# Moving a load, a normalization and two DMA groups within the queues of a 3-block transformer kernel

## Chip, cores and metric

The kernel runs on one core of a Trainium2 chip. The metric is the device time of one execution in microseconds (us), lower is better; three executions of a kernel are compared by their median. All matmuls run on TensorE (PE), elementwise work on VectorE (DVE), ScalarE (ACT) and GpSimd (POOL), and DMAs are issued from the queues of SyncE (SP), ScalarE and GpSimd.

## What is computed

One sequence of 512 tokens, width 1024, goes through two mixers (a gated delta rule, then a short convolution) and a third block: compressed, selected and windowed attention with a pooling and a gating branch, cross attention to a memory of 256 rows, and a gated feed-forward net. Everything is float32. Two places matter here:

```
# gated delta rule, chunks of 64 tokens, per head
a_mat = tril(kb k^T * decay, -1);  u, w = solve(I + a_mat, vb), solve(I + a_mat, kb * exp(g))
for each chunk: v_new = u - w S; o = q S + (qk) v_new; S = S * decay + k^T v_new
o = rms_norm(o, norm_w) * silu(z);  y = o @ w_out

# third block
x = x + rms_norm(concat(attention, pool, gate) @ w_out_2)
m = rms_norm(mem_2)            # 256 rows of 1024
x = x + rms_norm(cross_attention(rms_norm(x) @ w_mq, m @ w_mk, m @ w_mv) @ w_mo)
```

## The kernel before

Activations lie transposed in SBUF (8 tiles of 128 channels by 512 tokens). Each weight matrix is cut into slabs of 256 columns (128 partitions by 2048 floats, 1 MB). SP loads the slabs in a fixed order into a ring of two slots. For most of them the float32 product is made of three products of rounded parts: ACT writes the high part `w_hi` of a slab (`split_hi`, L1516), DVE or POOL writes the low part `w_lo = ring - w_hi` (`split_lo`, L2114 and L2847), and PE multiplies hi by hi, hi by lo and lo by hi (L740 to L742). `w_hi` and `w_lo` have two places each, so the high part of slab n+2 can only be written when PE has used up slab n.

Every engine runs its own instructions in the order in which the program issues them. Semaphores tie the engines together; a wait in a queue, the SP queue too, holds up all that stands behind it.

**The delta rule** works on 4 groups of 4 heads (g = 0 to 3). In each group ACT writes the decay factors (L1746), DVE multiplies them into `A_T` (L2408, counted by `a_ready`) and `QK_T` (L2410). The diagonal blocks of 16 by 16 of A are then inverted by DVE in another layout: four DMAs from SP (L556) and four from ACT (L1752) write the blocks to `blocks_d` in DRAM, SP reads them back (L558), DVE inverts them (`invert_blocks`, L2373 and L2376), SP writes `inverses_d` (L564), and four DMAs each from SP (L569) and ACT (L1766) bring the inverses back. PE waits for those and goes on with transposes (L1063). From g = 1 on, the RMS norm of the outputs of the group before is worked in between: ACT sums squares of its last chunk (`out_squares`, L1699), DVE makes means of them (`out_means`, L2340 and L2345), ACT takes the roots (`out_roots`, L1709 and L1711), and DVE scales the outputs (`scaled_outs`, L2354), before it starts `invert_blocks(g)`. PE turns the scaled outputs (L987) once DVE has also read its banks (`vb_ready`, L2418).

**The attention's output projection** has 4 slabs, called XOUT to XOUT+3. Its 8 output tiles (`mix_proj(c)`, c = 0 to 7) use one slab for two tiles. The first 4 tiles are accumulated at L1367 to L1369, from `mix_start` on, while the attention still runs; the last 4 are at L740 to L742. After tiles 3 to 6 PE transposes two tiles each of the memory rows (L1403); the first of these waits for `mem_scaled`. The memory's norm consists of the load `mem_rows` (L666), two squares with row sums, a Ln and an Exp on ACT (L1995 to L1999, ends with `mem_rstd`), and two scalings on DVE (L2757, L2758, end with `mem_scaled`). The load writes into a part of SBUF that the attention uses, so it waits for `attT_out`, the end of the attention. `post_norm` squares and copies the eight output tiles as PE finishes them (ACT L1534 and L1548, DVE L2150 and L2153); at even tiles it first runs `ahead`, the split of slab XOUT+2 or XOUT+3, and after each tile `beside(k)`.

Of the kernel before, what the change touches and what calls it, by code (L numbers as in the profile page):

```python
# [8 lines left out]
D = 1024  # L9
P = 128  # L10
KD = D // P
NT = S // P
# [79 lines left out]
def build(nc, x, pre_norm_w, post_norm_w, gdn_w_in, gdn_conv_w, gdn_A_log, gdn_dt_bias, gdn_norm_w, gdn_w_out,  # L92
# [5 lines left out]
    ALU, ACT, AX = mybir.AluOpType, mybir.ActivationFunctionType, mybir.AxisListType  # L98
    ds = bass.ds
    ctx = ExitStack()  # L100
    with ctx:
# [24 lines left out]
        small = sb("small", P, 64)  # L126
        inv_count = sb("inv_count", P, 32)[:, :]
        eps = small[:, 0:1]
# [83 lines left out]
        v_of = [xT[:, 4:8, :], gate_out[:, 12:16, :]]  # L212
# [100 lines left out]
        XOUT = len(plan)  # L313
# [141 lines left out]
        MT, HD = MEM // P, D // MH  # L455
# [4 lines left out]
        mem_rows, at = cut(at, MT, D)  # L460
# [3 lines left out]
        mem_junk = mem_T.rearrange("p k m -> p (k m)")[:, 0:D]  # L464
# [58 lines left out]
        def _(sp):  # L523
# [134 lines left out]
            for n in range(4):  # L658
                o = slice(256 * n, 256 * n + 256)
                load_parts([(lambda r, f=f: r[64 * f:64 * f + 64, 0:1024].rearrange("d (k c) -> d k c", c=256),  # L660
                             w_out_2[0, 256 * f:256 * f + 256, o].rearrange("(k d) c -> d k c", d=DH)) for f in range(2)]
                           + [(lambda r: r[:, 1024:SLOT].rearrange("p (k c) -> p k c", c=256),
                               w_out_2[0, 512:D, o].rearrange("(k p) c -> p k c", p=P))])
                if n == 3:
                    sp.wait_ge(attT_out, NT)
                    sp.dma_start(mem_rows, mem_2[0].rearrange("(t p) c -> p t c", p=P)).then_inc(mem_in, 16)  # L666
            load(w_mk_2[0].rearrange("(k p) c -> p k c", p=P)[:, :, 0:256], wide(256))
# [21 lines left out]
            for a in range(2):  # L689
                for t in range(NT):  # L690
                    n = NT * a + t
# [807 lines left out]
        def _(act):  # L1499
# [194 lines left out]
            def out_squares(g, v_T, ts):  # L1694

                for t in ts:
                    act.wait_ge(scan_done, HG * (NCH * g + t + 1))
                    for h in range(HG):
                        ins = act.activation(squares_dump(g, h)[:, t * P:(t + 1) * P], v_T[:, h, t * P:(t + 1) * P], ACT.Square,  # L1699
                                             accum_out=ssq[:, 0, 4 * h + t:4 * h + t + 1])  # L1700
                        if h + t < HG + NT - 2:
                            own.did(ins)
                if ts[-1] == NT - 1:
                    ins.then_inc(l2_rms, 1)

            def out_roots(g):

                act.wait_ge(o_mean, g + 1)
                own.did(act.activation(ssq[:, 1, :], ssq[:, 1, :], ACT.Ln))  # L1709
                own.settle()  # L1710
                act.activation(ssq[:, 1, :], ssq[:, 1, :], ACT.Exp, scale=-0.5).then_inc(l2_rms, 1)  # L1711
# [13 lines left out]
            for g in range(GROUPS):  # L1725
# [17 lines left out]
                for h in range(HG):  # L1743
                    act.wait_ge(gb_done, 4 * g + h + 1)
                    for t in range(NT):
                        ins = act.activation(decay(g, h)[:, t * P:(t + 1) * P], psum[4 + h][:, t * P:(t + 1) * P],  # L1746
                                             ACT.Exp, bias=decay_bias(g)[:, t, h:h + 1])
                    ins.then_inc(decay_ready, 1)
                for b in rows_of_scalar:
                    r = slice(BLK * b, BLK * b + BLK)  # L1750
                    act.wait_ge(a_ready, HG * (g + 1))
                    act.dma_start(block_view(blocks_d, b), diagonal[0][r, :, r]).then_inc(blocks_moved, 16)  # L1752
                if g:
                    out_squares(g - 1, v_of[(g + 1) % 2], (NT - 1,))
                    out_roots(g - 1)
                for j in range(2):
                    act.wait_ge(kr_done, 2 * g + j + 1)
                    act.activation(k_rows[:, j, :], psum[4 + 2 * j][:, :], ACT.Copy).then_inc(kr_ready, 1)
# [231 lines left out]
                    if what == "c":  # L1990
                        out_columns(n)

            act.wait_ge(mem_in, 16)
            for t in range(MT):
                own.did(act.activation(mem_junk, mem_rows[:, t, :], ACT.Square, accum_out=small[:, 1 + t:2 + t]))  # L1995
                own.settle()
            own.did(act.activation(small[:, 1:3], small[:, 1:3], ACT.Ln, bias=eps, scale=1.0 / D))
            own.settle()
            act.activation(small[:, 1:3], small[:, 1:3], ACT.Exp, scale=-0.5).then_inc(mem_rstd, 1)  # L1999

            def mem_beside(k):

                if 3 <= k < 7:
                    for j in (2 * k - 6, 2 * k - 5):
                        act.wait_ge(mem_turned, j + 1)
                        act.activation(mem_T[:, j, :], psum[4 + j % 2][:, 0:MEM], ACT.Copy, scale=KVW(j)).then_inc(mem_turned_out, 1)
# [98 lines left out]
        def _(dve):  # L2105
# [3 lines left out]
            def split_lo(n, count=None):  # L2109

                if count is None:
                    dve.wait_ge(split_ready, plan[n]["splits"] - 1)
                dve.wait_ge(w_hi_ready, plan[n]["splits"] if count is None else count)
                dve.tensor_tensor(w_lo[:, plan[n]["pair"], :], ring[:, n % 2, :], w_hi[:, plan[n]["pair"], :].bitcast(F32), ALU.subtract)\  # L2114
                    .then_inc(split_ready, 1)
# [24 lines left out]
            def post_norm(y_T=y_T, parts=True, beside=lambda k: None, between=lambda k: None, ahead=lambda pair: None, second=None, summed=0):  # L2140

                layer = st["layer"]
                base = 8 * layer
                dve.wait_ge(h_ready, 8 * layer + 8)
                for k in range(KD - 1):
                    if k % 2 == 0:
                        ahead(k // 2)
                    dve.wait_ge(square_ready, base + k + 1)
                    if k == 0:
                        dve.tensor_copy(rs[:, :], sq[:, 0, :]).then_inc(square_used, 1)  # L2150
                    else:
                        dve.wait_ge(square_used, base + k)
                        dve.tensor_tensor(rs[:, :], rs[:, :], sq[:, k % 2, :], ALU.add).then_inc(square_used, 1)  # L2153
                    beside(k)
                if second is not None:
                    split_lo_halves(second)
                dve.wait_ge(rms_ready, 2 * layer + 1)
                if layer == 0:
                    dve.wait_ge(x_back, KD)

                def scaled(k):
                    ins = dve.tensor_tensor(y_T[:, k, :], y_T[:, k, :], rs[:, :], ALU.mult)
                    if k < summed:
                        ins.then_inc(x_ready, 1)
                    else:
                        own.did(ins)

                def added(k):
                    if k < summed:
                        return  # L2170
                    own.settle()
                    dve.tensor_tensor(xT[:, k, :], xT[:, k, :], y_T[:, k, :], ALU.add).then_inc(x_ready, 1)

                def low_part(k):
                    dve.wait_ge(h_hi_ready, 8 * layer + 8 + k + 1)
                    dve.scalar_tensor_tensor(out=h_lo[:, k, :], in0=xT[:, k, :], scalar=PRE[layer + 1](k), in1=h_hi[:, k, :].bitcast(F32),
                                             op0=ALU.mult, op1=ALU.subtract).then_inc(h_ready, 1)

                scaled(0)
                added(0)  # L2180
                for k in range(1, KD):
                    scaled(k)
                    if parts:
                        low_part(k - 1)
                    added(k)
                    between(k)
                if parts:
                    low_part(KD - 1)
                    dve.wait_ge(x_squared, 8 * layer + 8)
                    for far in (1, 2, 4):  # L2190
                        for k in range(0, KD, 2 * far):
                            ins = dve.tensor_tensor(y_T[:, k, :], y_T[:, k, :], y_T[:, k + far, :], ALU.add)
                            if far < 4:
                                own.did(ins)
                        if far < 4:
                            own.settle()
                    ins.then_inc(squares_summed, 1)
                st["layer"] += 1
# [554 lines left out]
                    if (what, s, n) == ("s", len(steps) - 1, 3):  # L2753
                        shares(s, n)

            dve.wait_ge(mem_rstd, 1)
            own.did(dve.tensor_scalar(mem_rows[:, 0, :], mem_rows[:, 0, :], small[:, 1:2], None, ALU.mult))  # L2757
            dve.tensor_scalar(mem_rows[:, 1, :], mem_rows[:, 1, :], small[:, 2:3], None, ALU.mult).then_inc(mem_scaled, 1)  # L2758

            def split_q0(k):  # L2760
                if k == 5:
# [1 line left out]
                    dve.tensor_tensor(w_lo[:, Q0["pair"], :], q0_slab, w_hi[:, Q0["pair"], :].bitcast(F32), ALU.subtract)\  # L2763
                        .then_inc(split_ready, 1)

            post_norm(between=split_q0, ahead=lambda pair: split_lo(XOUT + 2 + pair) if pair < 2 else None)
            split_lo(MEM0 + 4)
            norm_ready()
            q0 = plan[MEM0 + 3]["end"] - 2
# [155 lines left out]
```

## Time and profile before

| what | us |
|---|---|
| median of 3 executions (lowest, highest) | 1813.44 (1812.98, 1815.06) |
| the profiled execution's own time | 1813.44 |
| its span, first to last instruction | 1811.6 |
| PE busy | 1778.7 (98% of the span) |
| DVE, ACT, POOL busy | 992.5, 707.8, 159.6 |

The profile is of one execution. Its span is 1.84 us shorter than the time, which is what lies around it. Busy shares are means over stages; what a local change costs is read in the timeline of its stage. The mean granted TensorE clock is 0.998 of full speed.

### The profile page before, as it was taken

The numbers are of one execution on the slowest core, as the hardware profiler recorded it, in microseconds if no ns is written. First come the engines' busy times: TensorE is split into PE (matmuls) and PEld (weight loads), VectorE is DVE, ScalarE is ACT, GpSimd is POOL, SyncE is SP. The second block draws the span as 40 slices with busy tenths as digits, with TensorE's granted clock in tenths as the row PEclk, the third lists the DMA queues.
The fourth block names the chain that finished last, engine by engine and source line by source line (L and its number), as shares of the span: only waits on it lengthen the run. The fifth ranks groups of instructions, "written<-read, shape, count | busy, mean of one in ns | idle before, by whom it ended". The sixth has DMA issues, their size and how long they took to land.

```text
span 1811.6 us, 26512 instructions
## 1 busy us (share of the span) xinstructions
PE 1778.7 (98%) x10563; PEld 1439.0 (79%) x10563; DVE 992.5 (55%) x1677; ACT 707.8 (39%) x1333; POOL 159.6 (9%) x112
## 2 busy tenths in 40 slices
PE   8999999999999999999999999999999999999998
PEld 6778888887887888888888788478876778888887
DVE  4645646466636545444443656744333687778434
ACT  5644556456445221111134623754123532223323
POOL 1123131221002000000000101610000100000000
PEclk9999999999999999999999999999999999999999
DMA  6422212122234322333223451023222222332221
GB/s 193 83 61 65 67 48 77 54 71 61 100 109 106 117 93 93 93 101 106 94 93 94 91 117 47 24 70 112 98 70 93 70 93 94 106 101 93 93 76 65
DMA packets 183183, 158.18 MB, mean 87 GB/s; under 512 B 36977, under 2 KB 179886, under 8 KB 183050
## 3 DMA queue, kind: packets, MB, share of 16 engines
q1 hardware_dynamic: 172672, 152.88, 27.7%
q0 software_dynamic: 1248, 3.19, 1.2%
q10 hardware_dynamic: 9163, 0.72, 0.4%
q8 instruction: 70, 1.15, 0.3%
q14 instruction: 30, 0.25, 0.0%
HBM read 152.77 MB, written 3.73 MB: 86 GB/s over the span
## 4 chain that ended last, share of the span: by engine, by line
PE 87%; DVE 5%; ACT 4%; DMA 2%; issue 1%; ACTq 0%; SPq 0%; POOL 0%; DVEq 0%
PE bank L740 13%; PE bank L742 13%; PE bank L741 13%; PE bank L841 5%; PE bank L843 5%; PE bank L842 5%; PE bank L730 4%; PE bank L940 3%; PE bank L942 3%; PE bank L941 3%; PE bank L1063 1%; PE bank L1074 1%; PE bank L1085 1%; PE bank L1329 1%; DMA arena<-inverses_d 1%
## 5 line engine op out<-in xcount | busy, mean ns | idle before, releaser
L1516 ACT ACTIVATE w_hi<-ring 128x2048 fp32r<-128x2048 f32 x122 | 233.9, 1918 | 533.2 <-PE bank L742 376.2
L740 PE MATMUL bank<-h_hi,w_hi 128*128 128x512 f32 x1024 | 400.5, 391 | 2.2 <-DVE w_lo L2114 2.0
L742 PE MATMUL bank<-h_hi,w_lo 128*128 128x512 f32 x1024 | 398.5, 389 | 0.0
L741 PE MATMUL bank<-h_lo,w_hi 128*128 128x512 f32 x1024 | 398.4, 389 | 0.0
L2114 DVE TENSOR_TENSOR w_lo<-ring,w_hi 128x2048 fp32r<-128x2048 f32 x101 | 231.2, 2289 | 240.5 <-ACT w_hi L1516 240.5
L740 PEld LDWEIGHTS bank<-h_hi,w_hi 128*128 128x128 f32 x1024 | 192.2, 188 | 44.9 <-issue 3.6
L742 PEld LDWEIGHTS bank<-h_hi,w_lo 128*128 128x128 f32 x1024 | 192.2, 188 | 40.3
L741 PEld LDWEIGHTS bank<-h_lo,w_hi 128*128 128x128 f32 x1024 | 192.2, 188 | 40.0 <-issue 0.5
L2847 POOL TENSOR_TENSOR w_lo<-ring,w_hi 128x2048 fp32r<-128x2048 f32 x20 | 91.8, 4591 | 1043.9 <-ACT w_hi L1516 920.2
L841 PE MATMUL bank<-h_hi,w_hi 128*128 128x512 f32 x432 | 170.6, 395 | 1.6 <-DVE arena L2807 1.0
L843 PE MATMUL bank<-h_hi,w_lo 128*128 128x512 f32 x432 | 168.3, 390 | 0.0
L842 PE MATMUL bank<-h_lo,w_hi 128*128 128x512 f32 x432 | 168.2, 389 | 0.0
L940 PE MATMUL bank<-h_hi,w_hi 128*128 128x512 f32 x368 | 151.0, 410 | 0.0
L942 PE MATMUL bank<-h_hi,w_lo 128*128 128x512 f32 x368 | 143.9, 391 | 0.0
L941 PE MATMUL bank<-h_lo,w_hi 128*128 128x512 f32 x368 | 143.5, 390 | 0.0
L2213 DVE SCALAR_TENSOR_TENSOR arena<-arena,cols 128x511 f32<-128x511 f32 x120 | 90.1, 750 | 14.8 <-DVE arena L2213 0.3
L841 PEld LDWEIGHTS bank<-h_hi,w_hi 128*128 128x128 f32 x432 | 81.1, 188 | 18.3 <-issue 1.4
L843 PEld LDWEIGHTS bank<-h_hi,w_lo 128*128 128x128 f32 x432 | 81.1, 188 | 17.2
L842 PEld LDWEIGHTS bank<-h_lo,w_hi 128*128 128x128 f32 x432 | 81.2, 188 | 16.1
L942 PEld LDWEIGHTS bank<-h_hi,w_lo 128*128 128x128 f32 x368 | 69.1, 188 | 15.3
L940 PEld LDWEIGHTS bank<-h_hi,w_hi 128*128 128x128 f32 x368 | 69.2, 188 | 14.9 <-issue 1.9
L941 PEld LDWEIGHTS bank<-h_lo,w_hi 128*128 128x128 f32 x368 | 69.4, 188 | 11.9
(440 smaller groups left out, 2502.1 us busy)
## 6 DMA issues: line engine op xcount, KB each, us to landing
ring<-in_sc_w_in SPq DMA_DIRECT2D x32, 1024.0 KB, 5.3
ring<-in_gdn_w_in SPq DMA_DIRECT2D x24, 1024.0 KB, 5.4
ring<-in_w_up SPq DMA_DIRECT2D x22, 1024.0 KB, 5.0
ring<-in_gdn_w_out SPq DMA_DIRECT2D x8, 1024.0 KB, 5.2
ring<-in_sc_w_out SPq DMA_DIRECT2D x8, 1024.0 KB, 5.2
ring<-in_w_down SPq DMA_DIRECT2D x8, 1024.0 KB, 5.2
ring<-in_w_in SPq DMA_DIRECT2D x4, 1024.0 KB, 5.6
ring<-in_w_mk SPq DMA_DIRECT2D x4, 1024.0 KB, 5.2
```

Source lines behind the costliest of these rows:

```text
L740: pe.matmul(o, a_hi(k), b_hi(k), start=(k == tiles[0]), stop=False)
L741: pe.matmul(o, a_hi(k), b_lo(k), start=False, stop=False)
L742: mm = pe.matmul(o, a_lo(k), b_hi(k), start=False, stop=(k == tiles[-1]))
L841: pe.matmul(o, w_hi[:, st["slab"], w], h_hi[:, k, :], start=(a == 0 and k == 0), stop=False)
L842: pe.matmul(o, w_hi[:, st["slab"], w], h_lo[:, k, :], start=False, stop=False)
L843: mm = pe.matmul(o, w_lo[:, st["slab"], w], h_hi[:, k, :], start=False, stop=(a == last and k == kt - 1))
L940: pe.matmul(psum[b][:, :], w_hi[:, st["slot"], w], h_hi[:, k, :], start=(k == 0), stop=False)
L941: pe.matmul(psum[b][:, :], w_hi[:, st["slot"], w], h_lo[:, k, :], start=False, stop=False)
L942: mm = pe.matmul(psum[b][:, :], w_lo[:, st["slot"], w], h_hi[:, k, :], start=False, stop=(k == KD - 1))
L1516: act.activation(w_hi[:, plan[n]["pair"], :], ring[:, n % 2, :], ACT.Copy).then_inc(w_hi_ready, 1)
L2114: dve.tensor_tensor(w_lo[:, plan[n]["pair"], :], ring[:, n % 2, :], w_hi[:, plan[n]["pair"], :].bitcast(F32), ALU.subtract)\
L2847: pool.tensor_tensor(w_lo[:, plan[n]["pair"], :], ring[:, n % 2, :], w_hi[:, plan[n]["pair"], :].bitcast(F32), ALU.subtract)\
```

## The change

It has three edits. (1) SP's wait for `attT_out` and the load of `mem_rows` are issued after slab XOUT+1 in place of after slab XOUT+3. (2) In groups 1 to 3 of the delta rule, `out_squares` and `out_roots` stand before ACT's four block DMAs and no longer behind them. (3) The memory norm's part on ACT moves from ahead of `post_norm` to behind its output tile 0, and its part on DVE to behind tile 1. The instructions moved are the same ones.

```diff
@@ -661,7 +661,7 @@
-                if n == 3:
+                if n == 1:
                     sp.wait_ge(attT_out, NT)
                     sp.dma_start(mem_rows, mem_2[0].rearrange("(t p) c -> p t c", p=P)).then_inc(mem_in, 16)
@@ -1746,13 +1746,13 @@
                     ins.then_inc(decay_ready, 1)
+                if g:
+                    out_squares(g - 1, v_of[(g + 1) % 2], (NT - 1,))
+                    out_roots(g - 1)
                 for b in rows_of_scalar:
                     r = slice(BLK * b, BLK * b + BLK)
                     act.wait_ge(a_ready, HG * (g + 1))
                     act.dma_start(block_view(blocks_d, b), diagonal[0][r, :, r]).then_inc(blocks_moved, 16)
-                if g:
-                    out_squares(g - 1, v_of[(g + 1) % 2], (NT - 1,))
-                    out_roots(g - 1)
@@ -1990,16 +1990,16 @@
-            act.wait_ge(mem_in, 16)
-            for t in range(MT):
-                own.did(act.activation(mem_junk, mem_rows[:, t, :], ACT.Square, accum_out=small[:, 1 + t:2 + t]))
-                own.settle()
-            own.did(act.activation(small[:, 1:3], small[:, 1:3], ACT.Ln, bias=eps, scale=1.0 / D))
-            own.settle()
-            act.activation(small[:, 1:3], small[:, 1:3], ACT.Exp, scale=-0.5).then_inc(mem_rstd, 1)
-
             def mem_beside(k):
 
+                if k == 0:
+                    act.wait_ge(mem_in, 16)
...
                 if 3 <= k < 7:
@@ -2753,9 +2753,11 @@
-            dve.wait_ge(mem_rstd, 1)
-            own.did(dve.tensor_scalar(mem_rows[:, 0, :], mem_rows[:, 0, :], small[:, 1:2], None, ALU.mult))
-            dve.tensor_scalar(mem_rows[:, 1, :], mem_rows[:, 1, :], small[:, 2:3], None, ALU.mult).then_inc(mem_scaled, 1)
+            def mem_scale(k):
+                if k == 1:
...
@@ -2763,7 +2765,7 @@
-            post_norm(between=split_q0, ahead=lambda pair: split_lo(XOUT + 2 + pair) if pair < 2 else None)
+            post_norm(beside=mem_scale, between=split_q0, ahead=lambda pair: split_lo(XOUT + 2 + pair) if pair < 2 else None)
```

## Rows read from the trace of the kernel before

**Rows 1.** The page: busy us (share) and instructions of PE; the chain's shares.
```profile
PE 1778.7 (98%) x10563; PEld 1439.0 (79%) x10563; DVE 992.5 (55%) x1677; ACT 707.8 (39%) x1333; POOL 159.6 (9%) x112
...
PE 87%; DVE 5%; ACT 4%; DMA 2%; issue 1%; ACTq 0%; SPq 0%; POOL 0%; DVEq 0%
```

**Rows 2.** Waits of PE, whole span: releaser, us in total, times, longest.
```profile
PE bank L1063 <- DMA arena<-inverses_d: 4.0, 4, 1.4
...
PE bank L730 <- ACT arena L2055: 2.8, 1, 2.8
```

**Rows 3.** Timeline of PE, group 1: start, us, instruction, [idle before, releaser].
```profile
203.90 1.03 PE L1029 MATMUL bank<-masks,arena 128*128 128x128 f32 x8
...
214.34 1.91 PE L987 MATMUL bank<-masks,xT 128*128 128x128 f32 x16
217.30 1.97 PE L1063 MATMUL bank<-masks,arena 128*128 128x128 f32 x16 [1.05 <-DMA arena<-inverses_d]
```

**Rows 4.** Timeline of ACT, group 1.
```profile
198.22 1.86 ACTq L1752 DMA_DIRECT2D blocks_d<-arena  x4
200.12 0.31 ACT L1699 ACTIVATE arena<-xT 128x128 f32<-128x128 f32 x1 [2.66 <-issue]
...
202.04 0.21 ACT L1711 ACTIVATE arena<-arena 128x16 f32<-128x16 f32 x1
202.16 1.07 ACT L1758 ACTIVATE arena<-bank 128x512 f32<-128x512 f32 x2
```

**Rows 5.** Timeline of DVE, group 1.
```profile
200.51 0.16 DVE L2340 TENSOR_SCALAR arena<-arena 128x8 f32<-128x8 f32 x1
201.51 0.24 DVE L2345 SCALAR_TENSOR_TENSOR arena<-arena 128x8 f32<-128x8 f32 x2 [0.84 <-ACT arena L1699]
...
204.70 0.17 DVE L2373 TENSOR_TENSOR arena<-arena 128x15 f32<-128x15 f32 x1
```

**Rows 6.** Timeline of SP's queue, group 1.
```profile
201.51 0.34 SPq L558 DMA_DIRECT2D arena<-blocks_d  x1
```

**Rows 7.** Timelines of SP's queue and of DVE, group 0.
```profile
93.81 0.34 SPq L558 DMA_DIRECT2D arena<-blocks_d  x1
...
95.89 0.17 DVE L2373 TENSOR_TENSOR arena<-arena 128x15 f32<-128x15 f32 x1 [3.00 <-DMA arena<-blocks_d]
```

**Rows 8.** Timeline of PE, group 3.
```profile
433.00 1.97 PE L1063 MATMUL bank<-masks,arena 128*128 128x128 f32 x16 [0.72 <-DMA arena<-inverses_d]
```

**Rows 9.** Waits of SP's queue, whole span.
```profile
SPq L666 <- DVE h_lo L2719: 24.0, 1, 24.0
```

**Rows 10.** Timeline of ACT, output projection.
```profile
1207.94 1.06 ACT L1995 ACTIVATE arena<-arena 128x1024 f32<-128x1024 f32 x1 [5.63 <-DMA arena<-in_mem]
...
1210.63 0.20 ACT L1999 ACTIVATE small<-small 128x2 f32<-128x2 f32 x1
1212.88 1.92 ACT L1516 ACTIVATE w_hi<-ring 128x2048 fp32r<-128x2048 f32 x1 [2.04 <-PE bank L1369]
...
1215.74 0.60 ACT L1534 ACTIVATE sq<-bank 128x512 f32<-128x512 f32 x1
```

**Rows 11.** Timeline of DVE, output projection.
```profile
1210.87 0.76 DVE L2757 TENSOR_SCALAR arena<-arena,small 128x1024 f32<-128x1024 f32 x1 [7.83 <-ACT small L1999]
...
1217.66 0.69 DVE L2153 TENSOR_TENSOR rs<-rs,sq 128x512 f32<-128x512 f32 x1
```

**Rows 12.** Timeline of PE, output projection.
```profile
1218.07 0.60 PE L1403 MATMUL bank<-masks,arena 128*128 128x128 f32 x4
```

**Rows 13.** DMA issues, 1236 to 1247 us: KB each, us from issue to landing.
```profile
arena<-in_w_mq SPq DMA_DIRECT2D x1, 1024.0 KB, 5.3
ring<-in_w_mk SPq DMA_DIRECT2D x1, 1024.0 KB, 8.9
```

**Rows 14.** Windows of PE: stretch, its length, busy us (instructions), granted clock, DMA share, GB/s.
```profile
1377.00:1378.00 1.00, 1.00 (x2) 0.50 0.00 0
...
1379.00:1380.00 1.00, 1.00 (x2) 0.50 0.63 185
```

More of the change, by code:

```diff
@@ L1991, in _ @@
                         out_columns(n)
-            act.wait_ge(mem_in, 16)
-            for t in range(MT):
-                own.did(act.activation(mem_junk, mem_rows[:, t, :], ACT.Square, accum_out=small[:, 1 + t:2 + t]))
-                own.settle()
-            own.did(act.activation(small[:, 1:3], small[:, 1:3], ACT.Ln, bias=eps, scale=1.0 / D))
-            own.settle()
-            act.activation(small[:, 1:3], small[:, 1:3], ACT.Exp, scale=-0.5).then_inc(mem_rstd, 1)
-            def mem_beside(k):
+            def mem_beside(k):
+                if k == 0:
+                    act.wait_ge(mem_in, 16)
+                    for t in range(MT):
+                        own.did(act.activation(mem_junk, mem_rows[:, t, :], ACT.Square, accum_out=small[:, 1 + t:2 + t]))
+                        own.settle()
+                    own.did(act.activation(small[:, 1:3], small[:, 1:3], ACT.Ln, bias=eps, scale=1.0 / D))
+                    own.settle()
+                    act.activation(small[:, 1:3], small[:, 1:3], ACT.Exp, scale=-0.5).then_inc(mem_rstd, 1)
                 if 3 <= k < 7:
@@ L2754, in _ @@
                         shares(s, n)
-            dve.wait_ge(mem_rstd, 1)
-            own.did(dve.tensor_scalar(mem_rows[:, 0, :], mem_rows[:, 0, :], small[:, 1:2], None, ALU.mult))
-            dve.tensor_scalar(mem_rows[:, 1, :], mem_rows[:, 1, :], small[:, 2:3], None, ALU.mult).then_inc(mem_scaled, 1)
+            def mem_scale(k):
+                if k == 1:
+                    dve.wait_ge(mem_rstd, 1)
+                    own.did(dve.tensor_scalar(mem_rows[:, 0, :], mem_rows[:, 0, :], small[:, 1:2], None, ALU.mult))
+                    dve.tensor_scalar(mem_rows[:, 1, :], mem_rows[:, 1, :], small[:, 2:3], None, ALU.mult).then_inc(mem_scaled, 1)
             def split_q0(k):
```

## Prediction
> **What bounds the kernel now.** I read the page's busy line first: PE is busy for 98% of the span, and the chain of work that ended last runs over PE for 87% of it [rows 1]. So an edit on another engine can only matter where PE waits, or where it comes to wait. The second view is the list of PE's waits [rows 2]: the longest sum, 4.0 us in four pieces, is the wait for the inverted blocks at L1063, once in each head group. PE waits nowhere in the output projection. The reader should see from this that there is little to win: were the waits near the two edited places gone altogether, it would be about 4 us of 1813. What can be lost has no such limit, because everything PE loses goes straight into the time. The third view is the timeline of each engine at the two places [rows 3 to 7, 10 to 12]. I take the places one by one.
>
> **Edit 2, the order on ACT in groups 1 to 3.** Before, ACT issues its four block writes at 198.22 as soon as A is ready, which takes 1.86 us, and then squares, waits for DVE's means and takes the roots [rows 4]. SP starts to read the blocks back at 201.51 [rows 6], 3.29 us after ACT's first issue. How long that read takes until DVE can use it is seen in group 0, where DVE stood waiting for it: 95.89 - 93.81 = 2.08 us [rows 7]. In group 1 the blocks were therefore there at 201.51 + 2.08 = 203.59, and DVE began to invert them at 204.70 [rows 5], because it was still busy scaling outputs. The blocks had 1.1 us to spare.
>
> After the edit, the squares run while ACT used to wait for A, so DVE finds them ready. It waited 0.84 us for them before L2345 at 201.51; now L2345 starts right behind L2340 at 200.51 + 0.16, at about 200.70 [rows 5]. That is 0.81 us earlier, and the roots move with it: L1711 from 202.04 to 201.23. Scaling is earlier by the same, so DVE would be free for the inversion at 204.70 - 0.81 = 203.89. That is the gain in the edit.
>
> But the block writes now stand behind the roots in ACT's queue, and the roots wait for DVE's means, which DVE only makes after A_T and QK_T. ACT takes the next instruction 0.12 us after L1711 starts [rows 4], so the first block write is issued at 201.35 and not at 198.22: 3.13 us later. The same 3.29 us until SP reads, and 2.08 us until the data is there, give 201.35 + 3.29 + 2.08 = 206.72 for the start of the inversion, against 204.70: **2.02 us later**. The wait has moved from the outputs' scaling, which had 0.8 us of waiting in it, to the blocks, which had 1.1 us to spare and lose 3.1.
>
> Behind the inversion everything follows it at a fixed distance: SP writes the inverses, SP and ACT fetch them, and PE's L1063 was already waiting 1.05 us for just that [rows 3]. PE does have other work to meet there: the transposes L987 at 214.34 need DVE's `vb_ready` products, which follow the inversion, so they would end about 0.7 us later than before but still at 216.9, ahead of the inverses, now due at 217.30 + 2.02 = 219.32. Hence the full 2.02 us falls on PE. Also moved by the edit are ACT's copies L1758, from 202.16 to 201.35 + 1.86 = 203.21. PE needs the first of the two copies at 203.90 [rows 3] and it would be done at about 203.8; if it were a few tenths late, PE would lose nothing more, since it comes to wait for the inverses anyway. The split of the next slab behind them and the SiLU copies move by 1.05 us with slack of more than a microsecond each. Nothing else stands behind ACT's block writes; SP's own four writes and its queue wait for `blocks_moved` and slide by the same 3.1 us, then 2.0 us.
>
> PE waits for the inverses in each of groups 1 to 3, and the smallest of these waits is 0.72 us [rows 8]; the distances on ACT and DVE are the same within 0.1 us in groups 2 and 3. Group 0 is not edited. Sum: 3 x 2.02 = **6.1 us**. Bounds: if ACT's four writes, no longer beside SP's, land 0.3 us sooner, 5.2 us; if they are issued 0.3 us later than I place them, 7.0 us.
>
> **Edit 1, the load of the memory rows.** SP stood 24.0 us at the wait for the attention's end [rows 9] with both slabs XOUT+2 and XOUT+3 already issued before it. The wait is what sets the load's start, 1203.07, and not its place in the queue. So the load does not start earlier by anything. What the edit does is to move the two slabs behind that wait. They were loaded more than 25 us before they were needed; now they are issued from 1203.4 on, behind the memory rows, on the same queue. The rows land at 1207.94 as before [rows 10]. Two loads of 1 MB issued 0.4 us apart landed after 5.3 and 8.9 us [rows 13], so a second MB lands about 4.0 us behind the first: XOUT+2 at about 1212.0 and XOUT+3 at about 1216. ACT splits XOUT+2 at 1212.88, when PE has freed its place [rows 10]: 0.9 us to spare. XOUT+3 is wanted at about 1220. Cost taken: **0**. If the three parts of slab XOUT+2 land slower, up to 1.2 us comes on top; a gain is excluded, as the split waits for PE.
>
> **Edit 3, the memory's norm inside post_norm.** Before, ACT does it from 1207.94 to 1210.83 and DVE scales from 1210.87 to 1212.3, in time in which both then wait for PE [rows 10, 11]. PE asks for the result at 1218.07 [rows 12]: 5.8 us to spare. After, ACT first splits XOUT+2 (from 1212.88) and squares and copies tile 0. It gets to the norm at 1215.74, where the square of tile 1 stood [rows 10]. The norm takes 1210.63 + 0.20 - 1207.94 = 2.89 us, so the square of tile 1 starts at about 1218.55 and ends 0.6 us later. DVE's sum of that square (L2153, 0.69 us, at 1217.66 before [rows 11]) comes ahead of the scalings in the new order, so it runs from 1219.2 to 1219.85. The two scalings took 1.42 us from the first start to the second's end [rows 11]; they end at about 1221.25. PE, which asked at 1218.07, goes on at 1221.3: **3.2 us later**. Behind these, PE has its slabs ready: XOUT+2's low part is done at 1217.2, and XOUT+3's at about 1224, while PE needs it some 11 us after it resumes. The banks of tiles 0 and 1 are free before PE takes them. PE is then busy without a gap until the norm of the third block, so nothing gives the stall back. Bounds: 2.9 us if the sum over tile 1 is quicker by its start-up, 3.5 us if each of the four handovers takes 0.1 us more.
>
> **Sum.** 6.1 + 0 + 3.2 = 9.3 us on the profiled execution's 1811.6 us span and its 1813.44 us time, which is also the median of the runs shown: **1822.7 us**, or +0.5%. By the bounds alone 1821.5 to 1824.
>
> **Rivals.** *The clock falls in the new gaps.* After PE's longest wait, 2.8 us [rows 2], with little work just before it, the granted clock stood at 0.50, the 1.2 GHz level, for three one-microsecond windows and part of two more [rows 14], which costs 1.5 to 1.7 us. The new gap at L1403 is 3.2 us, between dense matmuls; the gaps before L1063 become 2.4 us each, behind sparse transposes. One fall gives 1824.3, four give 1829. For it speaks the length of the gaps; against it that PE is fully busy on both sides of the 3.2 us. The Trainium skill ("TensorE: Matmul & The Clock Gate", section "HAM oscillation — how this bites in real kernels") says that gaps in which the engine waits for DMAs let the clock drop to half, so that the next work starts slow each time; that this case's trace agrees for its longest wait is said above, and that rule in each new gap would give the 1829.
>
> *The slabs are late.* Three loads share the queue after 1203. If they share it evenly, all land at about 1214; the split, the norm behind it and PE's start then slip by 1.1 us: 1823.8. For it speaks the margin of only 0.9 us, against it that of two loads the first landed at 5.3 us, hardly later than one alone.
>
> *The blocks keep their place: not slower.* If the block writes did not bind the inversion, because SP's read came at the old time or DVE's scaling still ended later, only the gain would be left: the inversion 0.81 us earlier in three groups, -2.4 us, and with edit 3's +3.2 us the time would be 1814.2, no difference. It decides at the point where ACT's first block write comes earlier than 1.1 us after its old place. I find it 3.1 us after; against the rival speaks that the writes can't leave ACT's queue before the roots, whose means DVE only makes at 200.7.
>
> *The changed norm is no stall.* If DVE reached the scalings before PE, edit 3 would cost nothing: 1819.5. It would need 3.2 us that I don't see.
>
> **How the numbers follow.** Chances: forecast 0.66, clock 0.14, late slabs 0.10, edit 3 for nothing 0.04, blocks keep their place 0.06. The forecast's and the late slabs' cases fill 1821 to 1824.5, one or two falls of the clock reach 1827, and 1819 takes in edit 3 for nothing: 1819 to 1827. A change of under 0.2% (3.6 us) can't be told from none here. Only the case of the blocks ends there; even with edit 3 for nothing beside it the time would be 1811.0, still within that. Faster needs both and a further saving that I don't find: slower 0.93, same 0.06, faster 0.01.
>
> **What would show it.** In the changed profile: ACT's four block writes 3.1 us after A is ready in groups 1 to 3, DVE waiting about 2.8 us for `blocks_d` before L2373, and PE's wait at L1063 about 3 us in those groups and 1.4 in group 0. In the output projection: the load of the memory rows still at the end of the attention, DVE's scalings after 1219, and a new wait of PE at L1403 for them of 3.2 us. The prediction is wrong if PE's wait at L1063 doesn't grow, if slab XOUT+2 holds ACT up by more than a microsecond, or if the granted clock drops behind the new gaps.

## The result, and the profile after

The changed kernel takes 1830.71 us (median of 4 runs, 1828.8 to 1833.78) against 1813.21 us: the ratio is 1.0098, with a 95% interval of 1.0085 to 1.0111. The forecast was +9.3 us; it is +17.5 us. The direction and both places were right, and the size is nearly twice as large. 1830.7 lies outside the range of 1819 to 1827. The profiled execution shown below was quicker than all of these (1827.32 us, span 1825.5 us), which matters for how it is read.

First PE's waits, as in [rows 2]: releaser, us in total, times, longest.

```profile
PE bank L1063 <- DMA arena<-inverses_d: 9.1, 4, 3.6
PE bank L1403 <- DVE arena L2760: 3.0, 1, 3.0
...
PE bank L730 <- ACT arena L2055: 2.8, 1, 2.8
...
PE bank L987 <- DVE arena L2418: 1.3, 2, 0.8
```

The wait for the inverted blocks has grown from 4.0 to 9.1 us, and there are two that were not there, at L1403 and at L987. The wait at L730 is the old one. Now group 1: the timelines of ACT, which answers to [rows 4], of SP's queue [rows 6], and of DVE [rows 5]. DVE has finished the matrix A, whose blocks are to be written, at 197.42.

```profile
200.23 0.21 ACT L1709 ACTIVATE arena<-arena 128x16 f32<-128x16 f32 x1 [2.37 <-DVE arena L2345]
200.48 0.22 ACT L1711 ACTIVATE arena<-arena 128x16 f32<-128x16 f32 x1
200.48 1.81 ACTq L1755 DMA_DIRECT2D blocks_d<-arena  x4
202.34 1.09 ACT L1758 ACTIVATE arena<-bank 128x512 f32<-128x512 f32 x2 [1.64 <-issue]
```

```profile
197.46 1.80 SPq L556 DMA_DIRECT2D blocks_d<-arena  x4
203.54 0.34 SPq L558 DMA_DIRECT2D arena<-blocks_d  x1
```

```profile
206.58 0.18 DVE L2373 TENSOR_TENSOR arena<-arena 128x15 f32<-128x15 f32 x1 [3.35 <-DMA arena<-blocks_d]
```

ACT waits 2.37 us for DVE's means, and only then come the four block writes, at 200.48, 3.02 us after SP's. SP writes its blocks at 197.46 but reads them all back only at 203.54, where it did so 3.3 us after its first write before. DVE, which had no wait for blocks here, waits 3.35 us. PE's L1063 in groups 1, 2 and 3:

```profile
219.36 2.95 PE L1063 MATMUL bank<-masks,arena 128*128 128x128 f32 x16 [2.42 <-DMA arena<-inverses_d]
...
332.03 2.98 PE L1063 MATMUL bank<-masks,arena 128*128 128x128 f32 x16 [3.62 <-DMA arena<-inverses_d]
...
443.31 1.97 PE L1063 MATMUL bank<-masks,arena 128*128 128x128 f32 x16 [2.14 <-DMA arena<-inverses_d]
```

Two things matter. The waits are longer than in [rows 3] and [rows 8]. And the same 16 transposes, 1.97 us before, take 2.95 and 2.98 us behind the first two waits. The windows of PE around the first say why (stretch, length, busy us, granted clock, DMA share, GB/s): the clock falls to 0.50, the 1.2 GHz level, just behind the gap.

```profile
218.00:219.00 1.00, 0.00 (x0) 1.00 0.38 35
219.00:220.00 1.00, 0.64 (x6) 1.00 0.54 52
220.00:221.00 1.00, 1.00 (x8) 0.58 0.76 228
221.00:222.00 1.00, 1.00 (x7) 0.50 1.08 384
222.00:223.00 1.00, 1.00 (x58) 0.50 1.02 359
223.00:224.00 1.00, 1.00 (x28) 0.71 0.17 41
```

In the output projection, ACT's and DVE's rows answer to [rows 10] and [rows 11], and PE's to [rows 12].

```profile
1223.51 1.92 ACT L1516 ACTIVATE w_hi<-ring 128x2048 fp32r<-128x2048 f32 x1 [10.56 <-PE bank L1369]
...
1226.38 1.06 ACT L1998 ACTIVATE arena<-arena 128x1024 f32<-128x1024 f32 x1
...
1229.18 0.58 ACT L1534 ACTIVATE sq<-bank 128x512 f32<-128x512 f32 x1
```

```profile
1229.79 0.69 DVE L2153 TENSOR_TENSOR rs<-rs,sq 128x512 f32<-128x512 f32 x1 [1.60 <-ACT sq L1534]
1230.40 0.75 DVE L2759 TENSOR_SCALAR arena<-arena,small 128x1024 f32<-128x1024 f32 x1
1231.06 0.74 DVE L2760 TENSOR_SCALAR arena<-arena,small 128x1024 f32<-128x1024 f32 x1
```

```profile
1231.86 0.65 PE L1403 MATMUL bank<-masks,arena 128*128 128x128 f32 x4 [3.01 <-DVE arena L2760]
```

ACT waits for PE before the split of slab XOUT+2, not for a DMA; then the norm runs between tiles 0 and 1, DVE adds the square of tile 1 before it scales, and PE waits 3.0 us. That is the forecast, step for step, with a wait 0.2 us shorter. The clock did not fall behind this gap in this execution.

### The profile page after: what moved, and what is told of

Its sections match the earlier page's. It is cut to its first block, busy times and chain, and to the rows that moved or that the text cites. A ratio compares the mean times of both kernels' runs of the same rounds, so it can differ in the third digit from the quotient of the medians.

```text
span 1825.5 us, 26512 instructions
## 1 busy us (share of the span) xinstructions
PE 1784.0 (98%) x10563; PEld 1441.3 (79%) x10563; DVE 992.6 (54%) x1677; ACT 707.9 (39%) x1333; POOL 159.2 (9%) x112
## 4 chain that ended last, share of the span: by engine, by line
PE 86%; DVE 6%; ACT 4%; DMA 3%; issue 1%; ACTq 0%; SPq 0%; POOL 0%; DVEq 0%
PE bank L740 13%; PE bank L741 13%; PE bank L742 13%; PE bank L841 5%; PE bank L843 5%; PE bank L842 5%; PE bank L730 4%; PE bank L940 3%; PE bank L942 3%; PE bank L941 3%; PE bank L1063 1%; PE bank L1074 1%; DMA arena<-inverses_d 1%; PE bank L1085 1%; PE bank L1329 1%
```

## The experiments

**The edits one by one, and edit 2 with PE kept busy.** The four kernels were timed side by side against the kernel before (1813.08 us, 21 runs). Edits 1, 2 and 3 are their hunks of the diff alone. The fourth has in addition:

```diff
                     turn_outs(g - 1, v_of[(g + 1) % 2], banks_read=4 * g)
+                    pe.wait_ge(*taken(12 * g + 8))
+                    keep_clock(0, 9)
```

> Edit 1 alone. Zero by the forecast: the load is issued when the attention ends, in both orders, and the two slabs land before ACT wants them. The rival (slabs late) gives +0.3 to +1.2 us, with ACT waiting for a DMA ahead of L1516 at slab XOUT+2. The load of the memory rows starting earlier than the end of the attention would refute my reading of the queue.

Edit 1 alone: 1813.2 us, ratio 1.0001 (0.9992 to 1.0009). It does nothing that can be told from noise, and no ACT wait for a slab appears.

> Edit 3 alone, with the load of the memory rows where it was. The order theory gives +3.0 us (PE's wait at L1403 in the changed kernel's profile) with the clock at 0.998. The clock theory gives +4.7 us in those runs in which the clock falls behind that wait. If the slabs' late load (edit 1) had a part in the stall, this is under 3 us.

Edit 3 alone: 1818.64 us, 1.0026 (1.0017 to 1.0036), on the means +4.8 us. The wait at L1403 is 3.01 us as in the full change. So edit 1 has no part in it. But the runs fall in two sorts: four lie at 1816.0 to 1816.9, six at 1818.6 to 1820.7. The listed mean clocks are 0.997 to 0.998 in the four and 0.995 to 0.997 in the six. The profiled one is of the second sort and shows a fall of the clock behind the new wait:

```profile
1222.24 1.12 PE L1403 MATMUL bank<-masks,arena 128*128 128x128 f32 x4 [3.01 <-DVE arena L2760]
```

```profile
1221.00:1222.00 1.00, 0.00 (x0) 0.98 1.09 386
1222.00:1223.00 1.00, 0.76 (x4) 0.50 0.64 220
```

The same wait of 3.01 us, behind which the transposes took 0.65 us above and take 1.12 us here. So the clock can fall behind this gap or not. That it fell there in all six of the slower runs is not shown, since only one of them was profiled.

> Edit 2 alone. The order theory (the blocks are late by 2.0 us in groups 1 to 3, which PE pays each time) gives +6.1 us, and if the clock falls behind the longer gaps at 1.7 us a fall, two to four falls make it +9.5 to +13 us. The clock theory is right only if the granted clock of the runs is below that of the kernel before (0.998) by about 0.001 for each fall; if the clock stays at 0.998 and the time is still over +9 us, the excess lies in late landings of DMAs. In the changed kernel's profiled run PE stood 10.6 us behind the kernel before when the attention ended, so I expect at least that here.

Edit 2 alone: 1824.93 us, 1.0066 (1.0051 to 1.0081), on the means +12.3 us. The mean granted clock of its runs is 0.9945, against 0.9977 for the kernel before. In its profiled execution the 16 transposes at L1063 take 3.25, 3.52 and 3.10 us in groups 1 to 3: three falls.

> Edit 2 alone, and PE fills the wait before L1063 in groups 1 to 3 with nine matmuls of 128 by 512 into a free bank (about 2.1 us, in time in which it would wait for the inverses). The clock theory: the clock doesn't fall, the time is under that of edit 2 alone by 3 to 6 us and comes to about +6 to +7.5 us over before, clock 0.998. The rival (the excess over 6.1 us is late DMAs, the clock is nothing): no difference from edit 2 alone.

With the fill: 1822.08 us, 1.0047 (1.0034 to 1.0061), on the means +8.5 us. The mean clock is back at 0.9978, and the transposes take 1.97 us again in all three groups:

```profile
214.85 2.32 PE L778 MATMUL bank<-exact 128*128 128x512 f32 x9
217.47 1.97 PE L1065 MATMUL bank<-masks,arena 128*128 128x128 f32 x16 [0.29 <-DMA arena<-inverses_d]
```

Both halves of the expectation need a word. The clock theory holds: matmuls whose result nobody reads give 3.8 us back on the means (12.3 - 8.5). The intervals of the two ratios overlap, so it is the clock readings and the row lengths that carry this more than the two times. But 8.5 us is left, over the +6 to +7.5 us that I expected. There is a second excess, which is not the clock.

**The whole change filled, and edit 3 filled.** Both have twelve more matmuls ahead of the wait for `mem_scaled`:

```diff
                 if 3 <= c < 7:
+                    if c == 3:
+                        keep_clock(4, 12)
                     pe.wait_ge(mem_scaled, 1)
```

> All three edits, and PE fills its new waits: nine matmuls before L1063 in groups 1 to 3, twelve (about 2.7 us) before the first L1403. The order theory with the clock theory: the clock returns to 0.997 to 0.998 and only the waits remain, +9 to +12 us over before (edit 2 filled was +8.5, edit 3's wait is 3.0), so 5 to 8 us under the changed kernel's +17.5. The rival (the stalls cost what they cost, and the clock differs by chance) gives no difference from the changed kernel.

1826.61 us, 1.0072 (1.0058 to 1.0086), on the means +12.2 us against 1813.31 us (24 runs) of the kernel before, at a mean clock of 0.9976. The 10 listed runs of the changed kernel have 0.9935. This is just above what was expected (+9 to +12); by the medians it is +13.3 us.

> Edit 3 alone, with the twelve matmuls in the wait before the first L1403. The clock theory: every run is like the better runs of edit 3 alone, +3.0 to +3.5 us, and none shows the second step of 1.7 us that this edit alone had in about half of its runs. The rival (the fill changes nothing): +4.7 us as edit 3 alone.

1817.26 us, 1.0021 (1.0011 to 1.0032), on the means +3.8 us. The clock is 0.9976 against 0.9966 for edit 3 alone. PE's fill ended 0.3 us before the result came, so the wait was not lengthened. The spread is still 1815.1 to 1819.9 (the kernel before has 1811.4 to 1817.7), so my expectation that all runs would lie at +3.0 to +3.5 is missed; the times alone do not separate this run from edit 3 alone.

**Where edit 2's second excess is.** I measured the steps of the block chain from the start of SP's block writes, each from the rows of the timeline. This start is called A from here on; in the changed kernel's group 1 it lies 0.04 us behind the end of the matrix of that name. All figures are us after A, except the last two columns, which are lengths:

| kernel, group | ACT writes | read | inversion | L1063 | read to inversion | fetch of inverses to L1063 |
|---|---|---|---|---|---|---|
| before, 1 | 0.01 | 3.30 | 6.49 | 19.09 | (hidden) | 3.65 |
| before, 2 | 0.01 | 3.49 | 6.49 | 18.85 | (hidden) | 3.40 |
| before, 3 | 0.01 | 3.31 | 6.50 | 18.85 | (hidden) | 3.40 |
| edit 2, 1 | 3.03 | 6.08 | 9.23 | 22.03 | 3.15 | 3.85 |
| edit 2, 2 | 3.02 | 6.48 | 8.53 | 22.61 | 2.05 | 5.13 |
| edit 2, 3 | 3.03 | 6.08 | 9.29 | 21.71 | 3.21 | 3.46 |

ACT's writes are 3.02 us later (forecast 3.13), and group 2's inversion 2.04 us later (forecast 2.02). But in groups 1 and 3 the read took 3.2 and not 2.08 us, and in group 2 the fetch took 1.7 us more. With both reads at 2.08 us, the order alone would have made the inversion 1.7 us later in groups 1 and 3 (6.08 + 2.08 - 6.49), because SP's read followed ACT's first write after 3.05 and not 3.29 us. Together L1063 is 2.94 + 3.76 + 2.86 = 9.6 us later in edit 2's profiled execution, and 2.74 + 2.81 + 2.96 = 8.5 us in the filled one. In the trace of DMAs, a packet of 0.02 MB of the instruction queue q8 is first seen inside just these three transfers: 6.5 us after A in group 1, 19.7 in group 2 and 6.4 in group 3. (Packets were looked for in windows of 0.3 us; the times given are the windows' starts.) The DMA view of the changed kernel over group 3's read, 427.9 to 431 us, shows it beside a landing of 2.8 us:

```profile
q8 instruction: 1, 0.02, 1.9%
...
arena<-blocks_d SPq DMA_DIRECT2D x1, 128.0 KB, 2.8
```

By that view, the packet took 1.9% of the time of 16 DMA engines over 3.1 us, which is 0.9 us of one engine, about what the read lost. That the read's part on this engine stood behind the packet is a reading of these two figures and not shown by itself.

Before the change, the packets were first seen at 203.6 in group 1, behind the landing of the read (2.07 us after its issue, at 203.58), at 325.7 in group 2, just behind the fetch (L1063 starts at 325.61), and at 420.2 in group 3, behind the read. So edit 2 may have moved the transfers into the way of packets that used to miss them. Three kernels test it: edit 2 alone, with waits that are already met added to one engine's stream, so that only the place of later code changes.

```diff
+                if g == 1:                      # pad_act; pad_dve has the same in DVE's stream
+                    for _ in range(12):
+                        act.wait_ge(eps_set, 2)
...
                     pe.wait_ge(vb_ready, 4)
+                    for _ in range(24):         # pad_pe
+                        pe.wait_ge(eps_set, 3)
                     keep_clock(4, 10)
```

> Edit 2 alone, with 12 waits that are already met put into ACT's stream at the start of group 1; only the place of later instructions in ACT's program changes. The code theory: where edit 2 alone paid more than the forecast (block read to inversion 3.1 us in groups 1 and 3, fetch of the inverses to L1063 5.1 us in group 2), a packet of the instruction queue q8 lay in the way at A+6.5, A+19.7 and A+6.4 us. If those packets are ACT's code, they move by several us here and the three figures fall to about 2.1, 3.5 and 2.1 us. The rival (these landings are long because of the block traffic itself): the figures stay at 3.1, 5.1, 3.1.

> The same with 12 waits in DVE's stream. The code theory: if the packets are DVE's code, it is this run in which they move and the landings get short; otherwise as edit 2 alone. The rival: 3.1, 5.1 and 3.1 us as in edit 2 alone.

> The same with 24 waits in PE's stream, in group 0 before its fill matmuls. The code theory: if the packets are PE's code, it is this run in which they move, by about 2 us or more, and the landings that they hit get short or others get long; otherwise as edit 2 alone. The rival: 3.1, 5.1 and 3.1 us as in edit 2 alone.

One execution of each was taken: 1827.96, 1825.59 and 1824.8 us, beside 1812.19 us of the kernel before. The times say nothing at this size; the steps do. With ACT or DVE padded, group 2's fetch stays at 5.22 and 4.78 us and group 3's read at 3.16 and 3.34 us; the packets stay where they were to 0.8 us. With PE padded, two packets moved earlier. In group 3 it now comes at 426.8, 4.1 us after A, and meets ACT's block writes in place of SP's read. Timelines of edit 2 alone (first) and of PE padded (second), for ACT's writes, SP's read and DVE's start:

```profile
425.85 1.81 ACTq L1755 DMA_DIRECT2D blocks_d<-arena  x4
...
428.90 0.34 SPq L558 DMA_DIRECT2D arena<-blocks_d  x1
...
432.11 0.17 DVE L2373 TENSOR_TENSOR arena<-arena 128x15 f32<-128x15 f32 x1 [3.52 <-DMA arena<-blocks_d]
```

```profile
425.74 2.90 ACTq L1757 DMA_DIRECT2D blocks_d<-arena  x4
...
429.90 0.34 SPq L558 DMA_DIRECT2D arena<-blocks_d  x1
...
431.94 0.17 DVE L2375 TENSOR_TENSOR arena<-arena 128x15 f32<-128x15 f32 x1 [3.45 <-DMA arena<-blocks_d]
```

The writes take 1.1 us longer to issue, and the read falls from 3.21 to 2.04 us: the delay has moved with the packet. In group 0, the packet came at 105.4 during the fetch of the inverses, which took 4.68 us; PE padded, it comes at 102.0 during the write of the inverses, which goes from 1.74 to 3.61 us, while the fetch falls to 3.53. Groups 1 and 2, in which the packet moved by less than 0.3 us, kept long transfers (2.86 and 4.90 us). So the packets follow the place in PE's stream, as PE's code would, and one costs the transfer that it meets 0.6 to 1.9 us.

The traces of all thirteen kernels, the one before included, say the same. Of their 52 reads of the blocks, twelve had a q8 packet starting 0.48 to 1.12 us after the issue, and these landed after 2.67 to 3.31 us. The other 40 landed after 1.86 to 2.18 us, but for one with 2.64. Of the 52 fetches of the inverses, the 19 with such a packet inside took 4.31 to 5.22 us until L1063 and the 33 without one 3.37 to 3.98 us. The kernel before is among them: 4.66 us in group 0, with a packet, against 3.40 to 3.65 us. The rival, that the block traffic itself is slower after the edit, falls.

**Half of edit 2, and a fill in PE's old wait.** Of edit 2, one half costs no wait: the squares can run while ACT waits for A, if the roots stay behind the block writes.

```diff
+                if g:
+                    out_squares(g - 1, v_of[(g + 1) % 2], (NT - 1,))
                 for b in rows_of_scalar:
...
                 if g:
-                    out_squares(g - 1, v_of[(g + 1) % 2], (NT - 1,))
                     out_roots(g - 1)
```

> Only the half of edit 2 that costs no wait: the squares stand before ACT's block writes, the roots stay behind them. The order theory: the block writes are issued 0.4 to 0.5 us later than before and not 3.1, the roots come 0.6 to 0.8 us earlier, the inversion starts 0.6 us earlier in each of groups 1 to 3, and the time is 1.8 us under before (0.1%, at the edge of what five rounds can tell). The rival, that any move of the block writes in ACT's queue costs its own length: +1.3 us.

1811.84 us, 0.9993 (0.9984 to 1.0002), on the means -1.1 us. The interval includes no change. The trace shows the gain in its place: the inversion starts 5.68, 6.14 and 5.68 us after A, where it was 6.49, and ACT's writes are not late at all, since their issue begins beside the last square (197.79 with the square running from 197.69). I had expected 0.4 to 0.5 us there.

The second version also has eleven matmuls in PE's old wait before L730, ahead of `pe.wait_ge(mpT_out, m + 1)` of the last head:

```diff
                     h = m // 4
+                    if h == MH - 1:
+                        keep_clock(4, 11)
                     pe.wait_ge(mpT_out, m + 1)
```

> The squares first, as in the run beside it, and eleven matmuls (2.5 us) in PE's longest wait of the kernel before, 2.82 us ahead of the last L730 matmuls, behind which the clock fell to 0.50 for three microseconds. The clock theory: those L730 matmuls take 3.7 us in place of 5.4, so 1.7 us come on top of the 1.8 us of the squares: 3.5 us under before, 0.2%. The rival (the clock falls there for another reason than the wait): as squares first alone.

1811.12 us, 0.9989 (0.998 to 0.9998): just below the kernel before, by 0.1%. On the means -2.3 us of the expected 3.5 us came. The eight matmuls behind the fill take 3.70 us, where [rows 14] showed them at half the clock and the kernel before took 5.40 (first line before, second line with the fill):

```profile
1376.21 5.40 PE L730 MATMUL bank<-arena 128*128 128x512 f32 x8 [2.82 <-ACT arena L2055]
...
1375.59 3.70 PE L730 MATMUL bank<-arena 128*128 128x512 f32 x8 [0.31 <-ACT arena L2058]
```

But three profiled executions without this fill, those of edit 2 filled, of the whole change filled and of edit 2 with ACT padded, also have 3.70 us behind a wait of 2.82 us. The clock does not fall there each time, so a fill can't give the 1.7 us each time. Nor do the runs' mean clocks show a gain: they average 0.9975 with this fill, 0.9975 with the squares first alone, and 0.9979 in the kernel before. What this fill is worth on average is therefore not shown.

## Why the prediction was right or wrong

**What bounds the kernel, and the waits as the only way in:** right. What the rows account for stands in a wait of PE or right behind one.

**Edit 1 at nothing:** right. The load starts when the attention ends, in both kernels, and the slabs landed in time. The rival of late slabs falls: ACT's wait before that split has PE as its releaser, and the last part of XOUT+2 had landed 0.5 us before it (forecast 0.9). That rival was also priced too low. By the prediction's own 4.0 us for each further MB, three loads that share the queue evenly would all land at about 1216 and not at 1214; in the changed kernel the last of them landed 12.7 us behind the issue of the first, which is 1215.8 on that scale.

**Edit 3, 3.2 us of waiting:** right, 3.0 us measured; alone it costs 4.8 us on the means. The fill gave 1.0 us of the difference back, with the mean clock going from 0.9966 to 0.9976. The other 0.8 us is not explained; it is about the size of the uncertainty of these means.

**Edit 2, "2.02 us later" three times, 6.1 us:** the mechanism was right to 0.1 us at ACT's writes. The term was too small; 8.5 to 9.6 us were measured in the two profiled executions of this edit. The step that failed is "that read takes until DVE can use it is seen in group 0 ... 2.08 us" together with "the distances on ACT and DVE are the same": a transfer takes about a microsecond more when a packet of PE's code meets it. I took one read as the price of three, and gave the landings 0.3 us of play, when the edit moved the reads by 3 us and with them what they meet. In the kernel before, the reads of groups 1 to 3 landed after 2.05 to 2.07 us, because no packet came early in them; the price of 2.08 us was right there and wrong after the move. In its place stand 1.7, 2.0 and 1.7 us by the order, 5.4 in all, plus 1.1 us for the read in groups 1 and 3 and 1.7 us for the fetch in group 2, 3.9 in all. The order's part is smaller than the forecast's 6.1 us because SP's read followed 0.24 us closer, as the lower bound had allowed for.

**The clock at 0.14 as a rival:** this is the larger error. I wrote "one fall gives 1824.3, four give 1829" and held against it "that PE is fully busy on both sides". The rule that the rival rested on, which the Trainium skill states ("TensorE: Matmul & The Clock Gate", section "HAM oscillation — how this bites in real kernels": gaps in which PE waits for DMAs bring the clock down, so that the next work begins slow), held behind six of the eight new gaps, 2.1 to 3.7 us long, in the three profiled executions without a fill that were read for it (the changed kernel, edit 2, edit 3). Of the six gaps in which PE waits for a DMA it held behind five, and of the two at L1403, in which PE waits for DVE, behind one. Dense work on both sides did not prevent it: after the 3.01 us wait at L1403 it fell in one profiled execution and not in another. The trace agrees with the rule, but as a frequency, not as a certainty. The fills put its worth in this change at 12.3 - 8.5 = 3.8 us for edit 2, 4.8 - 3.8 = 1.0 us for edit 3, and 17.2 - 12.2 = 5.0 us for the whole, each from means with a few runs. The 17.2 is that of the 10 listed runs of the changed kernel.

**The sum.** Forecast 6.1 + 0 + 3.2 = 9.3 us. Measured: the order 8.4 (5.4 + 3.0), the packets 3 to 4, the clock about 5, together about 17 of 17.5 us. The packets' part is 3.9 us in edit 2's profile and 3.3 us in that of edit 2 filled, where L1063 is 8.5 us later in all. The first of the three was the forecast. The second was left out of the sum without a reason; the third stood beside it as a rival with a chance of 0.14.

**What stays open.** With only a few runs each, the split between packets and clock is good to about a microsecond. In one execution, the filled whole change, group 3's packet came early (421.7, ahead of ACT's block writes and of the read) without a pad; what besides PE's position sets the moment of a packet was not tried. That the clock caused no more than the filled runs gave back is also only bounded: a fill itself can end late, as it did in group 3, where PE had no wait left behind it.

## What to carry to other kernels

A wait that ends in PE is not priced by its own length alone: where it takes PE's idle stretch from 1 us to 2 or 3 us, add the chance of a clock fall behind it (here 1 to 2 us each), and ask for the clock of every run, not of the one that was profiled. A transfer's time read in one place of a trace holds only as long as it keeps clear of instruction packets (the q8 row of the DMA view). An edit that moves transfers by 3 us can move them into such a packet or out of one, so give each moved transfer about a microsecond in the upper bound. Before an item moves ahead of another in a queue, look at what it waits for: the squares could go ahead of the block writes for nothing, the roots behind them could not.

## What the runs showed that I had not expected

The packets that move with PE's stream (queue q8, 0.02 MB each) delay the transfer that they meet: read of 128 KB 3.2 against 2.0 us, four writes of 16 KB issued in 2.90 against 1.81 us, write of 128 KB 3.6 against 1.7 us. That instructions come in blocks of 16 KiB by DMA, and that the cost to the engine itself is mostly hidden, is stated by the Trainium skill ("Runtime: NRT & Kernel Launch", section "Instruction fetch mechanics"). The packets' size agrees. Whether PE's own stream was ever held up by one was not looked at; what they cost the data transfers beside them is measured above.

The clock is not the same in equal executions: behind the same 2.82 us wait at L730 it fell in nine of the twelve profiled executions of the kernels without a fill there, and behind the same 3.01 us at L1403 in one of two. The listed runs of one kernel go with it: of the 24 of the kernel before, those at a mean clock of 0.999 took 1811.4 to 1812.2 us and the one at 0.995 took 1817.65 us.
